# Hybrid mixer and experts block: state keys first in the mixer, selectors from token numbers in the experts' loop

## The reference

```python
m = W_out( sigmoid(G_a h) * HGRN2(h) + sigmoid(G_b h) * [RG-LRU(conv4(h)) * gelu(.)] )
h = LayerNorm(alpha * h + m)
h = LayerNorm(alpha * h + SharedSwiGLU(h) + sum_topk w_e SwiGLU_e(h))

# HGRN2, chunks of 64 frames, b = cumulative log f within the chunk, k = 1 - f
scores = einsum(q, k, exp(b_t - b_s), causal)
o = scores @ v + (q * exp(b)) @ S
S = exp(b_last) * S + (k * exp(b_last - b))^T @ v

# experts: 64 experts, top 6 of them for each token, inner width 256
y_e = (silu(x @ w_gate) * (x @ w_up)) @ w_down
acc[tokens of e] += weight * y_e
```

## Time and profile before

| what | us |
|---|---|
| median of 3 runs (1386.85 to 1388.29) | 1387.31 |
| the profiled execution, its own time | 1389.1 |
| the profiled execution, its span | 1387.3 |
| PE busy within the span | 1198.5 |
| DVE busy | 796.2 |
| ACT busy | 435.2 |
| POOL busy | 223.7 |
| mixer, about 60 to 592 | 8 heads of 64.5 |
| experts' loop, about 729 to 1354 | 36 iterations of 17.35 |

### The profile page before, as it was taken

One profiled execution on the slowest core, in us unless ns is written; L12 is line 12 of the kernel. 1 busy time (PEld: TensorE's weight loads), 2 busy tenths in 40 slices (PEclk: granted clock), 3 DMA queues, 4 the chain that ended last, 5 costly groups with the idle time before them and its releaser, 6 DMA issues. The chain is left out here.

```text
span 1387.3 us, 18887 instructions
## 1 busy us (share of the span) xinstructions
PE 1198.5 (86%) x6574; PEld 762.7 (55%) x6574; DVE 796.2 (57%) x1290; ACT 435.2 (31%) x695; POOL 223.7 (16%) x117
## 2 busy tenths in 40 slices
PE   1779798988979897997959999999999999999991
PEld 1669686877878686646424444444444444444440
DVE  7867767768686777543154444444444444444447
ACT  3445554645455455302002222222222222222220
POOL 2423233324232323100010000000000000000000
PEclk9889999999999998996979999999999999999996
DMA  5021212021130303067007999999999999999932
GB/s 228 8 119 35 91 34 91 34 91 66 59 118 7 125 0 121 0 256 304 0 29 296 396 391 389 389 383 403 394 387 399 389 390 400 393 397 381 386 137 106
DMA packets 49155, 299.12 MB, mean 216 GB/s; under 512 B 7776, under 2 KB 9184, under 8 KB 16624
## 3 DMA queue, kind: packets, MB, share of 16 engines
q1 hardware_dynamic: 43664, 278.95, 49.5%
q0 software_dynamic: 5472, 19.93, 4.9%
HBM read 294.65 MB, written 4.19 MB: 215 GB/s over the span
## 5 line engine op out<-in xcount | busy, mean ns | idle before, releaser
L417 PE MATMUL pair<-hT,w_parts 128*128 128x264 f32 (+1 forms) x2112 | 388.3, 344 | 16.1 <-PEq L403 16.1
L417 PEld LDWEIGHTS pair<-hT,w_parts 128*128 128x128 f32 x2112 | 328.9, 194 | 62.9 <-issue 19.6
L1105 PE MATMUL pair<-raw,xgT 128*64 128x512 f32 x1152 | 254.5, 594 | 0.0
L211 POOL TENSOR_TENSOR w_parts<-w_raw,w_parts 128x1024 fp32r<-128x1024 f32 x68 | 175.8, 2587 | 383.9 <-ACT w_parts L206 383.9
L1218 DVE TENSOR_TENSOR acc<-acc,pair 128x512 f32<-128x512 f32 x296 | 180.3, 682 | 18.0 <-PE pair L1124 18.0
L1105 PEld LDWEIGHTS pair<-raw,xgT 128*64 128x64 f32 x1152 | 83.2, 138 | 164.9 <-issue 164.9
L1140 PE MATMUL pair<-raw,aT 128*64 128x512 f32 x576 | 131.5, 598 | 17.1 <-ACT aT L1188 17.1
L1123 PE MATMUL pair<-y_hi,ST 128*128 128x512 f32 x296 | 123.0, 415 | 22.5 <-ACT xgT L1175 20.9
L1231 DVE TENSOR_TENSOR act_a<-act_s,pair 128x256 f32<-128x256 f32 x36 | 15.2, 421 | 218.2 <-ACT act_s L1183 218.2
L1253 POOL DMA_INDIRECT xg<-h_rows,idx x38 | 35.8, 941 | 597.1 <-DVE idx L1212 596.0
L1124 PE MATMUL pair<-y_lo,ST 128*128 128x512 f32 x296 | 116.1, 392 | 0.0
(11 more groups left out here) (263 smaller groups left out, 1328.0 us busy)
## 6 DMA issues: line engine op xcount, KB each, us to landing
raw<-in_w_gate_up SPq DMA_DIRECT2D x144, 1024.0 KB, 10.1
raw<-in_w_down SPq DMA_DIRECT2D x72, 1024.0 KB, 7.6
w_raw<-in_w_in SPq DMA_DIRECT2D x36, 1024.0 KB, 6.6
xin<-in_x SPq DMA_DIRECT2D x4, 512.0 KB, 5.3
ws_gu<-in_ws_gate_up SPq DMA_DIRECT2D x1, 2048.0 KB, 8.4
h_rows<-acc SPq DMA_DIRECT2D x4, 512.0 KB, 16.5
out<-acc SPq DMA_DIRECT2D x4, 512.0 KB, 2.6
lw<-in_lru_w SPq DMA_DIRECT2D x8, 128.0 KB, 4.1
```

Source lines behind the costliest of these rows:

```text
L211: pool.tensor_tensor(w[:, n % PARTS, 1], w_raw[:, n // 2, n % 2], w[:, n % PARTS, 0].bitcast(F32), ALU.subtract).then_inc(sem("w_lo_ready" ...
L417: last = pe.matmul(o, w[:, n % PARTS, pw, k * P:(k + 1) * P], hT[ph][:, k, of], start=(k == 0 and m == 0), stop=(k == KB - 1 and m == 2))
L1105: last = pe.matmul(GU[half[s], :], xgT[h][:, (KB // 2) * c + k, half[s]], raw[:, ring_slot(PAIR * h + s, c), k * 2 * F:(k + 1) * 2 * F], s ...
```

## The change

**Mixer.** The arguments of `k_st` are written first after the scan and given to ACT with a semaphore of their own (`kst_arg`). ACT takes their exponential ahead of all others (`kst_exp`). sigmoid(q) now goes to `q_in`, so that the argument of `eq` is written before q is taken. DVE multiplies `k_st` right after q, while ACT takes the other exponentials, and gives `kst_ready`; `qk_ready` is given after `k_in`. On PE, l is projected directly behind o; it waits only for `q_taken`. The turning of `k_st` follows it and waits for `kst_ready`; the scores now wait for `qk_ready` themselves. ACT takes l before it copies the turned keys.

**Experts' loop.** `ST` is no longer made by turning `Sb`. A new constant `tok_row` (the numbers 0 to 511 in each partition, one load) is compared with the slot's token number `idx_f` by one DVE instruction, 512 columns (`place`). `turn_slots`, ACT's copy and `ident_b` go. `turn_a` moves from behind `look_up` to right behind `turn_x`, and AT into the bank GU. The bank that is freed is a fifth one for the sums, and `scatter` waits for `xgT_ready` only before its fourth sum. DVE builds the next `Sb` and `ST` at the head of its iteration.

```diff
-                    pe.wait_ge(sem("qk_ready"), j + 1)
+                    pe.wait_ge(sem("q_taken"), j + 1)
+                    project(GL, BQ_).then_inc(pe_sem["l_done"], 1)
+                    pe.wait_ge(sem("kst_ready"), j + 1)
                     for t in range(TT):
                         pe.transpose(B4[:, t * P:(t + 1) * P], k_st[:, META + t * P:META + (t + 1) * P], ident[:])
                     pe.transpose(B7[0:META, 256:384], k_st[:, 0:META], ident[:]).then_inc(pe_sem["kt_done"], 1)
-                    pe.wait_ge(sem("q_taken"), j + 1)
-                    project(GL, BQ_).then_inc(pe_sem["l_done"], 1)
...
+                    act.wait_ge(sem("kst_arg"), j + 1)
+                    act.activation(k_st[:], k_st[:], ACT.Exp).then_inc(sem("kst_exp"), 1)
                     act.wait_ge(sem("args_ready"), j + 1)
...
-                    act.activation(k_st[:], k_st[:], ACT.Exp).then_inc(sem("exps_ready"), 1)
...
+                    v.wait_ge(sem("kst_exp"), j + 1)
+                    v.tensor_tensor(k_st[:], k_st[:], kk[:], ALU.mult).then_inc(sem("kst_ready"), 1)
...
-            def turn_slots(p, h):
-                pe.wait_ge(sem("aT_ready"), p + 1)
-                for t in range(TT):
-                    last = pe.transpose(TURN[:, t * P:(t + 1) * P], flat(Sb[h][:, t]), ident_b[:])
-                last.then_inc(sem("st_done"), 1)
-
...
                 for g in range(ADDS):
                     t, m = g // 2, g % 2
-                    pe.wait_ge(sem("sum_free"), ADDS * n + g + 1)
...
+                    if g == SHARED and next_x:
+
+                        pe.wait_ge(sem("xgT_ready"), 2 * n + 4)
+                    if g >= len(SUM):
+                        pe.wait_ge(sem("sum_free"), ADDS * n + g - len(SUM) + 1 + ADDS)
...
-                    pe.wait_ge(sem("sum_free"), ADDS * p + 4)
+                    pe.wait_ge(sem("sum_free"), ADDS * p + ADDS)
                     turn_x(1 - h, q + h)
-                    turn_slots(p, h)
-
-                    pe.wait_ge(sem("xgT_ready"), 2 * p + 4)
+                    turn_a(p)
                     scatter(p, 1 - h)
 
-                    pe.wait_ge(sem("a_ready"), p + 1)
+                    pe.wait_ge(sem("aT_ready"), p + 1)
                     look_up(p + 2, h, q + 1)
-                    turn_a(p)
                     down(p, h, q)
...
+            def place(p, h):
+
+                v.wait_ge(sem("look_free"), p + 1)
+                v.tensor_scalar(ST[h][:], tok_row[:], idx_f[h][:, 0:1], None, ALU.is_equal).then_inc(sem("ST_ready"), 1)
...
+                    build(p + 2, h, q + 1)
+                    place(p, h)
```

More of the change, by code:

```diff
@@ L533, in _ @@
                     act.wait_ge(pe_sem["q_done"], j + 1)
-                    act.activation(eq[:], BQ_[:, 0:T], ACT.Sigmoid, bias=c(C_BQ)).then_inc(sem("sigq_ready"), 1)
+                    act.activation(q_in[:], BQ_[:, 0:T], ACT.Sigmoid, bias=c(C_BQ)).then_inc(sem("sigq_ready"), 1)
                     split_hi(act, j, 6)
@@ L544, in _ @@
                         n = SUB * (i + 1)
-                        act.activation(k_in[:, i, :, 0:n], k_in[:, i, :, 0:n], ACT.Exp)
-                    act.activation(k_st[:], k_st[:], ACT.Exp).then_inc(sem("exps_ready"), 1)
+                        last = act.activation(k_in[:, i, :, 0:n], k_in[:, i, :, 0:n], ACT.Exp)
+                    last.then_inc(sem("exps_ready"), 1)
                     act.wait_ge(pe_sem["x_done"], j + 1)
@@ L554, in _ @@
                     split_hi(act, j + 1, 0)
+                    act.wait_ge(pe_sem["l_done"], j + 1)
+                    act.activation(gx[:], BQ_[:, 0:T], ACT.Identity, bias=c(C_BL)).then_inc(sem("l_taken"), 1)
                     act.wait_ge(pe_sem["kt_done"], j + 1)
@@ L557, in _ @@
                     act.activation(kT[:].rearrange("p t c -> p (t c)"), B4[:, 0:T], ACT.Copy).then_inc(sem("kt_taken"), 1)
-                    act.wait_ge(pe_sem["l_done"], j + 1)
-                    act.activation(gx[:], BQ_[:, 0:T], ACT.Identity, bias=c(C_BL)).then_inc(sem("l_taken"), 1)
                     split_hi(act, j + 1, 1)
@@ L635, in _ @@
                     bc = chunked(b[:, META:TA])
+                    st.add(v.tensor_tensor(chunked(k_st[:, META:TA]), bc[:, :, CHUNK - 1:CHUNK].broadcast_to([P, NCH, CHUNK]),
+                                           bc, ALU.subtract))
+                    v.tensor_tensor(k_st[:, 0:META], b[:, META - 1:META].broadcast_to([P, META]), b[:, 0:META],
+                                    ALU.subtract).then_inc(sem("kst_arg"), 1)
                     for i in range(NSUB):
@@ L658, in _ @@
                         n = SUB * (i + 1)
-                        st.add(v.tensor_tensor(k_in[:, i, :, 0:n], k_in[:, i, :, 0:n], kc[:, :, 0:n], ALU.mult))
-                    st(v.tensor_tensor(k_st[:], k_st[:], kk[:], ALU.mult))
-                    v.sem_inc(sem("qk_ready"), 1)
+                        ins = v.tensor_tensor(k_in[:, i, :, 0:n], k_in[:, i, :, 0:n], kc[:, :, 0:n], ALU.mult)
+                        if i < NSUB - 1:
+                            st.add(ins)
+                        else:
+                            ins.then_inc(sem("qk_ready"), 1)
                     v.wait_ge(sem("x_taken"), j + 1)
@@ L1048, in experts @@
     y_lo = sb("y_lo", [P, D], F32R)
-    ST = [sb(f"ST{h}", [P, TT, P], F32R) for h in both]
-    ident_b = sb("ident_b", [P, P], BF16)
-    GU, MIX, XT, Y = banks[0], banks[1], banks[2:4], banks[4:6]
-    SUM = (banks[6], banks[7], banks[2], banks[3])
-    AT, TURN = MIX[:, 0:2 * P], MIX.bitcast(BF16)[:, 2 * SLOTS * TT:4 * SLOTS * TT]
+    ST = [sb(f"ST{h}", [P, T], F32R) for h in both]
+    tok_row = sb("tok_row", [P, T])
+    GU, XT, Y = banks[0], banks[2:4], banks[4:6]
+    SUM = (banks[6], banks[7], banks[1], banks[2], banks[3])
+    SHARED = 3
+    AT = GU[:, 0:2 * P]
     ADDS = 2 * TT
@@ L1063, in _ @@
         def _(sp):
+            sp.dma_start(tok_row[:], a["tok_row"]).then_inc(sem("tok_row_here"), 16)
             with sp.Fori(1, quads(sp)) as q:
@@ L1184, in _ @@
                     take_x(p + 1, 1 - h)
-                    act.wait_ge(sem("st_done"), p + 1)
-                    act.activation(ST[h][:].rearrange("p t c -> p (t c)"), TURN, ACT.Copy).then_inc(sem("ST_ready"), 1)
                     act.wait_ge(sem("at_done"), p + 1)
@@ L1202, in build, with looked_up @@
                                 ALU.is_equal).then_inc(sem("S_built"), 1)
-            def looked_up(p, h):
+            def place(p, h):
+                v.wait_ge(sem("look_free"), p + 1)
+                v.tensor_scalar(ST[h][:], tok_row[:], idx_f[h][:, 0:1], None, ALU.is_equal).then_inc(sem("ST_ready"), 1)
+            def looked_up(p, h, after=None):
                 v.wait_ge(sem("look_done"), p + 1)
+                if after is not None:
+                    v.wait_ge(sem("ST_ready"), after + 2)
                 for s in both:
@@ L1217, in add_up @@
                     part = acc[:, g // 2, (g % 2) * 512:(g % 2 + 1) * 512]
-                    v.tensor_tensor(part, part, SUM[g % 4][:, :], ALU.add).then_inc(sem("sum_free"), 1)
+                    v.tensor_tensor(part, part, SUM[g % len(SUM)], ALU.add).then_inc(sem("sum_free"), 1)
             build(0, 0, 0)
             build(1, 1, 0)
-            v.tensor_copy(ident_b[:], ident[:]).then_inc(sem("ident_b_ready"), 1)
             looked_up(0, 0)
             looked_up(1, 1)
-            v.sem_inc(sem("sum_free"), 4)
+            v.sem_inc(sem("sum_free"), ADDS)
+            v.wait_ge(sem("tok_row_here"), 16)
             n_quads = quads(v)
@@ L1365, in layout @@
     w["e_col"] = (n % E).astype(np.float32).reshape(P, 1)
+    w["tok_row"] = np.broadcast_to(np.arange(T, dtype=np.float32), (P, T))
     w["steps64"] = np.broadcast_to(np.arange(1, 13, dtype=np.float32) * SLOTS, (P, 12))
```

42 lines of the change are left out of this document (16 added, 26 removed).

## The result

The changed kernel takes 1327.45 us in the median of four runs (1316.64 to 1335.59), the kernel before 1387.08 in the same session. The ratio is 0.956 [0.953, 0.959]: 60 us faster, where 100 were forecast, and outside the range given. The profiled execution is the slowest of the four, own time 1335.6, span 1333.8.

A forecast was written before the change was run, and what follows sets the result against it. PE was taken as the bound, with the DMA engines close behind. Mixer 50 plus experts' loop 50 gave 100 us off the profiled 1389.1, so 1289 profiled and 1287 in the median; range 1268 to 1316.

The forecast's parts named there:

- Steps (1) to (5): Mixer: l fills PE's hole, early `k_st` is ready, its turning is short, then gates wait for ACT's copy and `xc`.
- steps (3) to (5): Mixer: turning takes 0.5 us, ending near 410.5; gates then wait for ACT's copy (about 411.4) and `xc` (410.8 to 413).
- The sum (6): Mixer: gates start 7.1 to 5.4 us a head earlier, 6.3 taken; eight heads give 50 us (40 to 57).
- The rival that kept a hole at `xc`: Mixer: POOL blocks DVE in `k_in` and `xc`; a head gains 4 us instead of 6.3; 1305 us, chance 0.11.
- Loop, steps (1) to (4): Experts' loop: selector, fifth bank and `turn_a` save 1.8 us, DVE's comparison costs nothing; PE alone needs 15.6 us an iteration.
- Loop, step (5): Experts' loop: the gather is late next, issued 8.5 us after `turn_x`, leaving 7.1 us to land, against 8.15 before.
- Loop, step (6): Experts' loop: 6.8 MB need 16.0 us; gathers land in 6 to 8; mean wait 0.35, iteration 15.95, gain 50 us.
- the rival in which the gather becomes the bound: Experts' loop: each gather takes 8 us, the iteration 16.5, gaining 31 us; 1306 us, chance 0.14.
- every gather 7.95 us: Experts' loop: the lower bound of the gain, 0.85 us an iteration or 31 us, with every gather landing in 7.95 us.
- The slower-than-before rival: Experts' loop: gathers queued among loads land in 10.2 us every iteration, costing back the 100 us gained; chance 0.02.
- the three signs for being wrong: PE waiting for `raw` in the loop, gathers over 8 us in the median, or a mixer head staying above 60 us.

The follow-up runs named there:

- after: The changed kernel in its first measurement and profile, against the kernel before: 1327.45 us, ratio 0.956.
- the mixer half alone: The changed mixer with the old experts' loop, against the kernel before: 1333.94 us, ratio 0.961.
- the repetition's profile: Profile of the same changed kernel measured again without any edit, on the chip of the last experiments: 1315.05 us, ratio 0.950 to the kernel before.
- the kernel with the `memset`: The changed kernel plus a memset of 1024 columns on POOL ahead of each gather: 1424.49 us, ratio 1.027 to the kernel before.
- the filler run: The changed kernel plus eight extra turnings of the identity on PE ahead of `turn_x`: 1308.26 us, ratio 0.944 to the kernel before.

## Why the prediction was right in one half and wrong in the other

**Mixer: right.** Steps (1) to (5) held. The keys are ready at 317.7, 9.4 us before PE turns them; the turning is in the clear; the next wait is at the gates, released by `xc` in 15 of the 16 heads of after and of the mixer half alone. The gates start 2.4 us after the turning does (327.10 to 329.51), inside the 1.45 to 3.25 that steps (3) to (5) span. The sum (6) was 50; 53.8 was measured with the mixer part alone, and 44.3 in the profiled execution, in which the clock fell in three heads instead of one. One reason was misattributed. The forecast put l in the hole first and the early keys second; the run with l back behind the turning shows that the second does it all. The rival that kept a hole at `xc` had its mechanism right, since POOL does hold up DVE twice, but not its size: 1.7 us a head, which step (6) had in its own sum.

**Loop, steps (1) to (4): right.** They gave 15.6 us for PE alone, and 15.60 was measured where the gathers landed early (in the kernel without the down loads). The first sum stands 1.1 us after `turn_x` (810.57 against 809.44), was 2.0; `down` follows `look_up` without a wait.

**Loop, step (5): right in structure.** POOL's issue 8.5 us after `turn_x` was forecast and is 8.34 at the full clock, and the gather was named as what is late next.

**Loop, step (6): the failure.** It saw that the hole in the load queue would close and that gathers would then land "later, 6 to 8 us", and turned this into a mean wait of 0.35 us with 7.1 us of room. The median landing is 8.5 us, and the mean wait 1.28. By its own figures, 8.5 + 8.5 is 17.0 us, which is what the loop takes (17.14). So the rival in which the gather becomes the bound came true. It was given 0.14 and priced at 16.5, too cheap for two reasons. Its landing of 8.0 was under the 8.8 already seen once, and it had no term for the clock, 0.26 us an iteration on the mean. The terms: 17.14 - 15.95 = 1.19, times 36 is 43 us (41 in the table above). With the 6 us of slow clock in the mixer that is the 47 by which the profiled execution missed its 1289. In the repetition's profile the loop alone missed, by 26. The bound was wrong as well as the centre, for "every gather 7.95 us" was not the worst case that row could have given.

The evidence that misled was the median of 5.1 in "the same loop". It was a median under the very condition that the change removed, and the forecast itself had said so in step (6). The Trainium skill ("DMA: Bandwidth & Descriptors", "Queues, rings and completion order") says that an engine takes turns between its queues; by that the forecast had 7.6 us, which the measured 7.7 to 9.3 us beside loads come nearer to than 5.1 does. It should have been the centre. No run isolates this rule.

The slower-than-before rival needed landings of 10.2 us. The largest were 9.9, and even the kernel with the `memset`, at a median of 9.3, got to 1.027 only because POOL issued 1.1 us later and the clock fell. Its reason for being unlikely, the load queue that empties, failed all the same.

**What the profile was to show.** Gone from the turning: yes. A new wait of 1 to 3 us a head before the gates: yes. A head of 57.5 to 59.5: four of seven, 58.4 to 58.5. Gathers 15.6 to 16.5 us apart: no, 17.1. GB/s above 400: no, 387, since the engines idle when PE waits. Waits for `xg` of 10 us: no, 50. Of the three signs for being wrong one came in full, gathers over 8 us in the median, and one in part: three heads took over 60 us (64.6, 63.1 and 60.1), those in which the clock fell.

## What to carry to other kernels

Find the loop that the gather is part of, from its consumer back to its issue, and add up that loop's length with the landing that it will have once the change has filled the queues, not with today's median. If the sum comes within a microsecond of the new iteration, move the issue ahead of work that doesn't need it: here that was worth 28 to 40 us and took the spread of the runs away. Don't take the gather's lead over the next loads for granted either: issued 1.1 us later, it cost the kernel before 59 us, where 3 us of spare time had been counted on. And take every exposed wait in a busy PE stretch for more than its length, because the clock can fall behind it, as it did in a third of the long waits here.

## What the runs showed of the hardware

- **A gather's landing depends on its neighbours, not on its size.** The same 0.5 MB of rows took 4.3 us in the median with the engines drained, 5.0 to 5.1 well ahead of the next loads, and 7.7 to 9.3 beside loads of 1 MiB each. How busy the engines are on average does not tell it: 5.1 us went with 384 GB/s in the loop of the kernel before, 9.3 with 329. In the kernel before, a lead of 0.4 to 0.8 us instead of 1.5 over the next loads went with 7.7 instead of 5.1.
- **The clock can fall behind short waits.** Waits of 2.04 and 2.73 us in a PE stream otherwise without gaps were followed by stretches at a granted clock of 0.57 and 0.65; after 0.76 and 0.95 us it stayed at 1.00. The length of the one wait does not decide it: the clock stayed at 1.00 after 2.52 us in after and after 2.75 us in its repetition (the stretch from 865.25), and was 0.71 and 0.87 after waits of 1.67. The Trainium skill ("TensorE: Matmul & The Clock Gate", "HAM oscillation") describes such a fall for waits on transfers between groups of matmuls. The rows of after agree that it happens, and in the filler run, where PE had work of no use in most of the waits, the loop's clock was 1.00.
- **One core's DMA engines held 420 GB/s** for 500 us, reading weights from HBM while gathers ran, and PE did not wait for them. The Trainium skill's 358 GB/s for a core ("DMA: Bandwidth & Descriptors", "Where 436 GB/s comes from") is not a limit for this kernel, which runs on one core.

Left open: how the DMA engines divide their time between a gather and the loads beside it, and why only some of the waits of 1.7 to 2.8 us are followed by a slower clock.
